# Block attention of a two-block transformer kernel: probabilities turned by 32x32 squares on VectorE and by transfers through device memory, and each head's value product issued one head later

## The reference, cut to what matters

```
s = einsum('bqhd,bqkhd->bhqk', q, k_sel) * HEAD_DIM ** -0.5
s = where(valid, s, -inf)
p = softmax(s, axis=-1)
out = einsum('bhqk,bqkhd->bqhd', p, v_sel)
```

## Time and profile before

| | |
|---|---|
| median of 3 runs | 1549.55 us (1548.9 to 1550.58) |
| the profiled execution's own time | 1550.08 us |
| its span | 1547.9 us |
| PE busy | 1519.1 us, 98% of the span |
| DVE, ACT, POOL busy | 1129.6, 744.6, 654.1 us |
| granted clock of TensorE, mean | 0.998 of full speed |

### The profile page before, as it was taken

How to read it: one execution, slowest core, us unless ns; L and a number is a source line. 1 busy time by engine, 2 the same in 40 slices (tenths; PEclk the granted TensorE clock), 3 DMA queues, 4 the chain that set the end, 5 groups by cost and what they waited for, 6 DMA issues and landing times.

```text
span 1547.9 us, 20637 instructions
## 1 busy us (share of the span) xinstructions
PE 1519.1 (98%) x7186; PEld 1252.6 (81%) x7186; DVE 1129.6 (73%) x1849; ACT 744.6 (48%) x1259; POOL 654.1 (42%) x291
## 2 busy tenths in 40 slices
PE   9999999999999999999999999999999999999998
PEld 7888888777888877888888888777779887888887
DVE  6689999887775445776777759776744887677775
ACT  6553233344462345754444245554763745444444
POOL 3444444322334432144555545351543344555551
PEclk9999999999999999999999999999999999999999
DMA  5333333212143323333333123222002432333321
GB/s 210 100 123 97 100 96 95 82 55 69 55 148 96 95 82 109 108 97 97 97 109 104 53 94 97 82 82 68 26 31 87 145 115 90 97 106 109 96 95 55
DMA packets 40419, 145.26 MB, mean 94 GB/s; under 512 B 4484, under 2 KB 4612, under 8 KB 40072
## 3 DMA queue, kind: packets, MB, share of 16 engines
q1 hardware_dynamic: 39312, 140.47, 28.4%
q10 hardware_dynamic: 1016, 3.61, 0.7%
HBM read 141.95 MB, written 2.11 MB: 93 GB/s over the span
## 4 chain that ended last, share of the span: by engine, by line
PE 87%; DVE 5%; issue 3%; ACT 3%; POOL 1%; DMA 1%; SPq 0%; DVEq 0%; ACTq 0%; POOLq 0%
PE bank L656 85%; PE bank L766 1%; DMA w_raw<-in_stream 1%; DVE x_sq L2176 0%; DVE cq_rstd L2112 0%; PE bank L1214 0%; DVE bias L2258 0%; ACT w_hi L1437 0%; POOL w_lo L530 0%; POOL dn_rest L540 0%; POOL res L625 0%; DMA dn_raw<-in_stream 0%; ACT kT L1611 0%; PE bank L1387 0%; PE bank L1030 0%
## 5 line engine op out<-in xcount | busy, mean ns | idle before, releaser
L530 POOL TENSOR_TENSOR w_lo<-w_raw,w_hi 128x1024 fp32r<-128x1024 f32 x191 | 473.3, 2490 | 524.9 <-ACT w_hi L1437 524.6
L656 PE MATMUL bank<-a_hi,w_hi 128*128 128x512 f32 (+1 forms) x1120 | 445.4, 398 | 2.6 <-DVE a_lo L3040 1.8
L656 PE MATMUL bank<-a_hi,w_lo 128*128 128x512 f32 (+1 forms) x1120 | 432.1, 386 | 0.0
L656 PE MATMUL bank<-a_lo,w_hi 128*128 128x512 f32 (+1 forms) x1120 | 431.7, 385 | 0.0
L1437 ACT CAST w_hi<-w_raw 128x1024 fp32r<-128x1024 f32 x199 | 204.9, 1048 | 177.5 <-DMA w_raw<-in_stream 177.4
L656 PEld LDWEIGHTS bank<-a_hi,w_hi 128*128 128x128 f32 x1120 | 210.7, 188 | 49.5 <-issue 3.8
L656 PEld LDWEIGHTS bank<-a_lo,w_hi 128*128 128x128 f32 x1120 | 210.7, 188 | 45.3 <-issue 3.3
L656 PEld LDWEIGHTS bank<-a_hi,w_lo 128*128 128x128 f32 x1120 | 210.7, 188 | 42.5
L540 POOL TENSOR_TENSOR dn_rest<-dn_raw,dn_first 128x1024 fp32r<-128x1024 f32 x13 | 31.4, 2416 | 276.2 <-DVE f_lo L2562 276.2
L656 PE MATMUL bank<-dn_rest,f_hi 128*128 128x512 f32 x364 | 141.6, 389 | 0.0
L1707 ACT CAST dn_first<-dn_raw 128x1024 fp32r<-128x1024 f32 x54 | 55.7, 1048 | 167.1 <-DVE dn_raw L2495 167.1
(11 more groups left out here) (427 smaller groups left out, 2880.3 us busy)
## 6 DMA issues: line engine op xcount, KB each, us to landing
w_raw<-in_stream SPq DMA_DIRECT2D x199, 512.0 KB, 3.5
dn_raw<-in_stream SPq DMA_DIRECT2D x56, 512.0 KB, 3.6
res<-in_xT ACTq DMA_DIRECT2D x1, 2048.0 KB, 8.0
out_y<-res_tok SPq DMA_DIRECT2D x8, 256.0 KB, 2.0
x_raw<-in_xT SPq DMA_DIRECT2D x3, 512.0 KB, 8.3
mem_raw<-in_memT SPq DMA_DIRECT2D x1, 1024.0 KB, 11.8
mrow<-m_rows ACTq DMA_DIRECT2D x4, 256.0 KB, 3.1
w_raw<-in_stream SPq DMA_DIRECT2D x2, 256.0 KB, 3.7
```

What stands on the lines that cost most here:

```text
L530: nc.gpsimd.tensor_tensor(w_lo[:, j, :], w_raw[:, j, :], w_hi[:, j, :].bitcast(F32), ALU.subtract).then_inc(w_lo_done, 1)
L656: return nc.tensor.matmul(o, l, r, start=start, stop=stop)
```

## The change: what it does

Only the 32 units of the first block's attention and what stands around them change; the later attentions get new counts for a semaphore. What becomes of a unit:

- The scores have four PSUM banks instead of two, since no turned squares pass through PSUM.
- DVE scales the probabilities and then turns them by 32x32 squares into `d_parts`. PE's 80 transposes and ACT's 32 copies of the turned squares are gone.
- After the fourth unit of a head SP writes `d_parts` (640 KB) to device memory, waits until it has landed, and reads it back in four transfers into `d_turned`, so that the squares stand where a full transpose would have put them.
- `d_parts` has one buffer: the first turn of the next head waits for the write.
- PE multiplies a head's values all at once, one head later; the last head's between 7/8 of AO0 and 7/8 of AO1.
- On ACT the exponential of unit n+2 stands ahead of the hook instead of behind it. `res` is loaded again after the squares.

```
+            def turn_parts(G):
+                sp.wait_ge(sems["pT_ready"], 4 * G + 4)
+                sp.dma_start(p_parts[G], d_parts[:, :, :, :].rearrange("p g k j -> p (g k j)")).then_inc(sems["p_stored"], 16)
+                sp.wait_ge(sems["p_stored"], 16 * (G + 1))
+                if G > 0:
+                    sp.wait_ge(sems["pv_done"], 4 * G)
+                rows = p_parts[G].rearrange("(g i) (h n) -> h i g n", g=RING, h=RING)
+                for h in range(RING):
+                    sp.dma_start(d_turned[PART * h:PART * h + PART, :, :, :].rearrange("i g k j -> i g (k j)"), rows[h]
+                                 ).then_inc(sems["p_landed"], 16)
+            first = CH["ATT"] + 8
+            rings(RING, first // RING * RING)
+            for c in range(first // RING * RING, first + 1):
+                ring(c)
+            for G in range(HEADS):
+                turn_parts(G)
+                ring(first + 2 * G + 1)
+                ring(first + 2 * G + 2)
...
-            attend(DSA_G, HEADS, dsa_score,
-                   lambda G, kb: values[:, kb, G * P:(G + 1) * P], dsa_hook)
+            def dsa_scores(n):
+                G, qb = n // 4, n % 4
+                if n >= RING:
+                    pe.wait_ge(sems["p_ready"], n - RING + 1)
+                dsa_score(G, qb, ps[4 + n % RING][:, 0:(qb + 1) * P]).then_inc(sems["s_ready"], 1)
+            def dsa_values(G):
+                pe.wait_ge(sems["p_landed"], 16 * RING * (G + 1))
+                if G > 0:
+                    pe.wait_ge(sems["o_ready"], G)
+                for qb in range(TB):
+                    for kb in range(qb + 1):
+                        m = mm(ps[2][:, qb * P:(qb + 1) * P].rearrange("p (g j) -> p g j", g=RING),
+                               values[:, kb, G * P:(G + 1) * P], d_turned[:, :, part_of(qb, kb), :], kb == 0, kb == qb)
+                    m.then_inc(sems["pv_done"], 1)
+            dsa_scores(0)
+            dsa_scores(1)
+            for n in range(4 * HEADS):
+                if n + 2 < 4 * HEADS:
+                    dsa_scores(n + 2)
+                dsa_hook(n)
+                if n % 4 == 3 and n >= 7:
+                    dsa_values(n // 4 - 1)
...
             pe.wait_ge(evac_act, DVE_FROM)
+            pe.wait_ge(sems["p_ready"], 4 * HEADS)
             ln_total(1)
+            ao_chunk(0, range(HEADS - 1))
+            dsa_values(HEADS - 1)
+            ao_chunk(1, range(HEADS - 1))
+            ao_chunk(0, range(HEADS - 1, HEADS))
+            ao_chunk(1, range(HEADS - 1, HEADS))
+            for j in range(2, KB):
+                ao_chunk(j, range(KB))
                 if j == LN_VAR_AFTER:
                     ln_total(2)
```

On ACT and on DVE:

```
-            attend(DSA_G, HEADS, dsa_hook)
-            act.wait_ge(sems["pv_done"], 4 * X_G)
-            act.dma_start(res[:, :, :], xT).then_inc(x_again, 16)
+            def dsa_exps(n):
+                act.wait_ge(sems["s_masked"], n + 1)
+                if n >= 2:
+                    act.wait_ge(sems["pT_ready"], n - 1)
...
+            for n in range(4 * HEADS):
+                if n + 2 < 4 * HEADS:
+                    dsa_exps(n + 2)
+                dsa_hook(n)
+                if n % 4 == 0 and n >= 8:
+                    head_hi(n // 4 - 2)
+            head_hi(HEADS - 2)
...
                 if k == 4:
+                    head_hi(HEADS - 1)
                     round_to(CH["AO"] + 1)
+            act.dma_start(res[:, :, :], xT).then_inc(x_again, 16)
...
+            def dsa_turn(n):
+                G, qb, b = n // 4, n % 4, n % 2
+                dve.wait_ge(sems["p_inv"], n + 1)
+                p = d_probs[b][:, 0:(qb + 1) * P]
+                V.tensor_scalar(p, p, rowinv[:, b:b + 1], None, ALU.mult).then_inc(sems["p_scaled"], 1)
+                dve.wait_ge(sems["p_scaled"], n + 1)
+                if G > 0 and qb == 0:
+                    dve.wait_ge(sems["p_stored"], 16 * G)
+                V.transpose(d_parts[:, :, part_of(qb, 0):part_of(qb, qb) + 1, :].rearrange("p g k j -> p k g j"),
+                            p.rearrange("p (k g i) -> p k g i", g=RING, i=PART)).then_inc(sems["pT_ready"], 1)
...
+            for n in range(4 * HEADS):
+                dsa_inverse(n)
+                dsa_turn(n)
+                if n % 4 == 1 and n >= 9:
+                    out_lo(n // 4 - 2)
+                if n + 2 < 4 * HEADS:
+                    dsa_mask(n + 2)
+                dsa_hook(n)
+            out_lo(HEADS - 2)
...
+                if k == 5:
+                    out_lo(HEADS - 1)
```

More of the change, by code:

```diff
@@ L101, with part_of @@
 RING = 4
+PART = 32
+TRIANGLE = 10
+def part_of(qb, kb):
+    return qb * (qb + 1) // 2 + kb
 AHEAD = 3
@@ L182 @@
 squares_added ssq_added ssqg_added start_hi start_ready start_scaled stat_ready stat_root tap_done
-topk_step uq_out vm_rows wi_copied wi_turned x2_done x2_gained apart_hi apart_lo dn_sum dn_done dn_evac b_sum b_cast b_ready z_done z_root y_written half_done half_rooted half_sums part_sq part_ssq qk_tanh post_tree post_sq first_w first_x
+topk_step uq_out vm_rows wi_copied wi_turned x2_done x2_gained apart_hi apart_lo dn_sum dn_done dn_evac b_sum b_cast b_ready z_done z_root y_written half_done half_rooted half_sums part_sq part_ssq qk_tanh post_tree post_sq first_w first_x p_stored p_landed
 """
@@ L266, in program @@
         spread = at("spread", [P, TB, P], TMP0 + 8192)
+        d_probs = [at(f"d_probs{i}", [P, T], C0 + 14336 + 16384 * i) for i in range(2)]
+        d_parts = at("d_parts", [P, RING, TRIANGLE, PART], TMP0 + 2048)
+        d_turned = at("d_turned", [P, RING, TRIANGLE, PART], TMP0 + 7168)
         x_raw = at("x_raw", [P, KB, T], G0)
@@ L364, in program @@
         m_rows = nc.dram_tensor("m_rows", [ML_HEADS, T], F32, kind="Internal").ap()
+        p_parts = nc.dram_tensor("p_parts", [HEADS, P, RING * TRIANGLE * PART], F32, kind="Internal").ap()
         def col(name, i=0, n=1, p0=0, p1=P):
@@ L463, in _ @@
             sp.dma_start(consts[:, :], consts_in).then_inc(consts_landed, 16)
-            sp.dma_start(mem_raw[:, :, :], memT).then_inc(mem_landed, 16)
+            sp.dma_start(mem_raw[:, :, :], memT).then_inc(sems["late_landed"], 16)
             def ring(c):
@@ L481, in left, with rings @@
                                  ).then_inc(dn_landed[LEFT.index(name)], 16)
[L483 to L488, removed]
+            def rings(first, last):
+                with sp.Fori(first // RING, last // RING) as i:
+                    for j in range(RING):
+                        sp.wait_ge(chunk_done, RING * i + j - (RING - 1))
+                        sp.dma_start(w_raw[:, j, :],
+                                     stream[bass.ds(RING * i + j, 1), :, :].rearrange("o p n -> (o p) n")
+                                     ).then_inc(raw_landed[j], 16)
+            def turn_parts(G):
[16 more added lines that the diff above has]
+                ring(first + 2 * G + 2)
+            then = first + 2 * HEADS + 1
+            for c in range(then, (then + RING - 1) // RING * RING):
+                ring(c)
+            rings((then + RING - 1) // RING * RING, CH["FF1"] // RING * RING)
             for c in range(CH["FF1"] // RING * RING, CH["FF1"]):
@@ L761, in turn @@
                     pe.wait_ge(sems["p_scaled"], U + 1)
-                    if U >= 2:
-                        pe.wait_ge(sems["pT_copied"], U - 1)
+                    if n >= 2:
+                        pe.wait_ge(sems["pT_copied"], n - 1)
                     for kb in range(keys_of(G, qb) // P):
@@ L770, in values_out @@
                     U, G, qb = 4 * G0 + n, G0 + n // 4, n % 4
-                    pe.wait_ge(sems["pT_copied"], U + 1)
+                    pe.wait_ge(sems["pT_copied"], n + 1)
                     if qb == 0 and G > 0:
@@ L919, in _, with ao_chunk @@
             pe.wait_ge(evac_act, DVE_FROM)
+            pe.wait_ge(sems["p_ready"], 4 * HEADS)
             ln_total(1)
-            for j in range(KB):
+            def ao_chunk(j, ks):
                 c, o = CH["AO"] + j, O["AO"] + j
-                chunk(c, c % RING, o, o % RING, c_hi, c_lo, ready=sems["o_ready"] if j == 0 else None)
+                chunk(c, c % RING, o, o % RING, c_hi, c_lo, ready=sems["o_ready"] if j == 0 else None, ks=ks)
+            ao_chunk(0, range(HEADS - 1))
[5 more added lines that the diff above has]
+                ao_chunk(j, range(KB))
                 if j == LN_VAR_AFTER:
@@ L1210, in latent_turn @@
                 pe.wait_ge(sems["p_ready"], U0 + n + 1)
-                pe.wait_ge(sems["pT_copied"], U0 + n)
+                pe.wait_ge(sems["pT_copied"], 4 * XH + n)
                 for kb in range(n % 4 + 1):
@@ L1218, in latent_values @@
                 h, nk = n // 4, n % 4 + 1
-                pe.wait_ge(sems["pT_copied"], U0 + n + 1)
+                pe.wait_ge(sems["pT_copied"], 4 * XH + n + 1)
                 if n % 8 == 0:
@@ L1267, in wo_step @@
                     elif j == 1:
```

(45 more changed lines are left out.)

1 line of the change is left out of this document (removed).

## The result

The change makes the kernel slower: 1589.01 us (median of 4 runs, 1587.56 to 1590.85) against 1549.67 us, a ratio of 1.0254 (95% interval 1.0237 to 1.0270), or +39.3 us. The forecast was 1572 (1558 to 1582): the side is right, the size is not. The profiled execution took 1587.56 us with a span of 1585.8; before, 1550.08 with 1547.9.

A forecast was written before the change was run, and what follows sets the result against it. The prediction took PE, busy 98% of the span, as the bound. It added 1.0 (start), 3.25 (next head), 10.0 (four heads) and 8.2 (tail), 22.4 us, to 1550.1: 1572.5, stated as 1572, range 1558 to 1582.

The forecast's parts named there:

- PE's saving: Each attention head: removing PE's turned blocks saves 0.88 us, less 0.22 of lost cover, net 0.66 if nothing else waits.
- VectorE's turn: Each head: VectorE's transposes of the four units take 0.30, 0.42, 0.55 and 0.68 us, some 1.95 a head.
- What the store does: Each head: store behind a 512 KB load lands at A + 5.5, next head's scores start at A + 13.2; +2.5 us a head.
- A: The moment when PE's half chunk in a head's last unit ends, for which SP's second ring waits.
- Period 19.65: Steady heads: one head takes 19.65 us against 17.15, +2.5 each, +10.0 over four heads.
- From those scores to the next A: PE's piece from a head's first scores to its last unit's half-chunk end: 0.25 + 0.22 + 2.76 + 0.44 + 2.76 = 6.4 us.
- The fall of the clock: Rival: PE's waits near 4 us drop the clock to 1.2 GHz for half a half chunk, +8 to +10, 1581; chance 0.18.
- if the clock row falls: Sign in the profile after: clock expected at 1.00; a fall of that row would show the forecast wrong.
- First stretch: Up to the scores of unit 8: six VectorE turns, one remainder fewer, cast ahead of key copy; +1.0 us (-1 to +2.5).
- Tail: From the scores of unit 28 to `ln_total(2)`: 50.8 us instead of 42.6, +8.2.
- AO0's late end: Tail: AO0 done after 39.1 us; AO4's load, cast and POOL's remainders then delay VectorE's sums, `ln_total(2)` at 50.8.
- The term for what comes behind: Behind `ln_total(2)`: what follows hangs on it as before, so nothing was added.

The follow-up runs named there:

- two-piece kernel: After with store ahead of second ring, key copy first, tail squares first, memory scaling moved, taps evened, plus the store split in two: 1543.15 us, the fastest measured.
- first tail experiment: After with store ahead of second ring and key copy first (1562.87 us), plus all eight layer-norm squares ahead of AO4's cast on ScalarE: 1554.49 us.
- single move in either list: After with one move: SP's store ahead of the second ring, 1564.42 us; or ScalarE's cast and key copy ahead of the exponential, 1566.86 us.
- same deal of taps: Late taps evened: 1565.33 us against 1562.87 with early store and key copy first; with the store also in two pieces, 1543.15 against 1550.32 for the old deal.
- store early: After with one move: SP issues a head's store ahead of the second ring, which waits for PE, instead of behind it: 1564.42 us.

## Why the prediction was right and wrong

- **PE's saving** (0.66 a head): right; 17.15 - 16.45 = 0.70 where nothing else waits (the two-piece kernel).
- **VectorE's turn** (0.30, 0.42, 0.55, 0.68 us): right; the four shapes took 0.31, 0.45, 0.58 and 0.71. The Trainium skill, page "VectorE: DVE Perf Modes", section "The three transpose paths", has 311 ns for 128x128 in bf16; this trace has the same for fp32.
- **What the store does** (the store at A + 0.35, landed at A + 5.5, scores at A + 13.2): right step by step. 0.41, 5.95 and 13.43 in the head shown; the store took 5.5 us against 5.15.
- **Period 19.65**: here it failed, and by one term: "From those scores to the next A", put at 6.4 us, which is its length at 2.4 GHz. The six measured 8.13, 8.86, 8.01, 9.18, 7.98 and 7.79, together 11.2 more than six of 6.45. With PE kept busy through the wait the period was 19.8. The fall of the clock stood among the rivals with 0.18, at +8 to +10 us and 1581; it should have been part of the forecast, since the forecast itself made PE stand for 4 us. Its own list of signs has "if the clock row falls", and the row fell. Beside waits of at most 0.5 us, the clock's 1.00 in the attention of the kernel before said nothing about waits of 4. Further on, that kernel's trace does have a fall, which the rows of the prediction don't show: 0.73 from 1108.7 to 1115.0 us, behind a wait of 1.05. The rule of the Trainium skill that stands with this rival (page "TensorE: Matmul & The Clock Gate", section "Part 1: The HAM clock gate"), that the throttled state is the default and activity releases it, was the better guide; by that rule, the trace agrees.
- **First stretch** (+1.0; measured +2.6): the direction was right, the term too small. The parts that it names come to 0.6 (2.7 - 0.69 + 0.95 - 2.4), and the rest of its 1.0 has no reason given. On its chain stands a scaling that took 1.80 us (308.77) beside a remainder of POOL's, instead of 0.29.
- **Tail** (+8.2; measured +10.0, of which 1.3 is the clock in the first piece): right, and by its own steps: PE waited 1.82 us for the taps (forecast 1.3), 0.78 for the loads (0.8) and 5.23 at `ln_total(2)` (3 to 5). AO0 ended 41.2 us after the scores of unit 28 against 39.1, and from there it was 11.3 us to `ln_total(2)` against 11.7. But it was read as the price of AO0's late end. The first tail experiment shows that it took the order of ScalarE's list to make it one: there AO0's end is as late, and the wait at `ln_total(2)` is gone. The term for what comes behind was nothing; the low clock behind that wait cost 2.4 us.

The terms: 22.45 forecast + 11.2 clock in the pieces + 1.6 start + 1.1 other time in the five heads + 0.4 in the tail + 1.1 behind it (2.4 for the low clock behind `ln_total(2)`, 1.6 less for the dip that only the profiled execution of the kernel before had, 0.3 not traced) = 37.9. Of the 15.4 us that the forecast lacked, the low clock behind the new waits is 13.6; the rest nearly cancels (1.6 + 1.1 + 0.4 + 0.3 - 1.6).

The forecast read the path, but not what was on it by choice. A key copy that needed none of this work stood behind it, and a single move in either list was worth 22 to 25 us.

The five heads' other 1.1 us are the way from A to the scores: 0.1 to 0.3 us a head longer than forecast, 13.43 against 13.2 in the head shown. What stays open: the tail's 0.4 was not traced further, and why some waits of 1 to 3 us are followed by a low clock and some aren't was not tried.

## What to carry to other kernels

When a forecast says that TensorE will stand for some microseconds, price the work behind each wait at the lower clock as well: here each wait of 4 to 7 us cost a further 1.3 to 2.7 us of slow products. Before moving work to an idle engine, write down what each engine's list puts behind the new wait, and take out what doesn't need it: the copy that feeds the busiest engine goes ahead of everything that depends on a transfer, and a store goes out in pieces so that its buffer is never waited for as a whole. Judge a repair in the kernel where its neighbour's wait is already gone; the same deal of taps was a loss of 2.5 us in one and a gain of 7.2 in the other.

## What the runs showed of the hardware

- **The clock behind a wait.** In after and the experiments made on it, all twelve key-copy waits of 3.46 to 7.25 us were followed by 5 to 12 products 0.43 us apart, then 0.23; behind key-copy waits of 0.3 to 1.6 us there were none. Of fifteen waits of 1.83 to 2.83 us nine were followed by slow products and six were not, one of 1.83 among the nine and one of 2.83 among the six: the length of the wait alone doesn't tell. Nor does the place: behind a wait of 1.05 us the kernel before has six products 0.43 us apart (1108.93 to 1111.47), and behind the same wait of 1.05 us in after (1148.12) the granted clock was 1.00. Useless products over the wait kept the clock at 1.00.
- **VectorE beside POOL.** The scalings of `d_probs`, between two SBUF tiles, take 0.29 to 0.49 us. Where one began in the first 0.8 us of a remainder of POOL's (2.4 to 2.8 us long), it took 1.8 to 2.5 and ended within 0.3 us of the remainder's end; scalings that began up to 0.3 us ahead of a remainder took 0.28 to 0.42. The fastest kernel has it too (its timeline of VectorE, then of POOL; the second remainder runs from 391.70 to 394.10):

```profile
388.88 2.33 DVE L2424 SCALAR_TENSOR_TENSOR bank<-conv_in,cols,bank 128x512 f32<-128x512 f32 x3
...
391.92 2.34 DVE L2497 TENSOR_SCALAR d_probs<-d_probs,rowinv 128x256 f32<-128x256 f32 x1
...
387.81 2.44 POOL L575 TENSOR_TENSOR w_lo<-w_raw,w_hi 128x1024 fp32r<-128x1024 f32 x1 [10.18 <-ACT w_hi L1515]
391.70 2.40 POOL L575 TENSOR_TENSOR w_lo<-w_raw,w_hi 128x1024 fp32r<-128x1024 f32 x1 [1.45 <-ACT w_hi L1515]
```

  Three taps, which read one operand from PSUM, took 0.78 each just before, though the first remainder ran until 390.25. The Trainium skill, page "SBUF — State Buffer", section "SBUF: two separate sides", tells of a port pair shared by the two engines, held for a whole instruction by whoever starts first; the trace agrees.
- **Transfers through device memory.** The same 640 KB took 5.5 us behind a 512 KB load and 3.2 with nothing ahead (medians; with the store early single ones took 2.6 to 4.9); in pieces, 3.1 for 384 KB and 2.7 for 256 KB. Reading the turned squares in a strided pattern cost PE nothing: a head's ten blocks of values went from 370.62 to 372.85, 0.22 each, as before.
